# Branch sums moved from VectorE to GpSimd, a third merged block turned by VectorE, filling matmuls left out, and a new order at the turn of the layers

## What is computed

```python
def hybrid_layer(x, ...):
    proj = rms_norm(x, pre_g) @ w_in            # q,k,v,z / u,b,c,z / q,k,v,z / three gates of 2048
    o_a = dilated_mixture_attn(q_a, k_a, v_a) * silu(z_a)          # 12 heads x 128
    o_c = b_c * causal_short_conv(c_c * u_c, conv_w, conv_b) * silu(z_c)
    o_r = normed(retention(q_r, k_r, v_r)) * silu(z_r)             # 12 heads x 128
    merged = (sigmoid(g_a) * (o_a @ w_branch_a) + sigmoid(g_c) * (o_c @ w_branch_c)
              + sigmoid(g_r) * (o_r @ w_branch_r))
    return x + rms_norm(merged @ w_out, post_g)
```

## Time and profile before

| | before |
|---|---|
| median of 3 runs | 2747.36 us (2747.34 to 2747.78) |
| the profiled execution | 2747.18 us, its span 2745.3 us |
| PE busy | 2734.2 us |
| DVE busy | 1923.9 us |
| ACT busy | 1221.6 us |
| POOL busy | 27.5 us |
| DMA | 529.10 MB, 193 GB/s mean |
| mean granted TensorE clock | 0.999 |

### The profile page before, as it was taken

One profiled execution on the slowest core, in us unless ns is written; L12 is line 12 of the kernel. 1 busy time (PEld: TensorE's weight loads), 2 busy tenths in 40 slices (PEclk: granted clock), 3 DMA queues, 4 the chain that ended last, 5 costly groups with the idle time before them and its releaser, 6 DMA issues.

```text
span 2745.3 us, 30445 instructions
## 1 busy us (share of the span) xinstructions
PE 2734.2 (100%) x12270; PEld 2269.6 (83%) x12270; DVE 1923.9 (70%) x2558; ACT 1221.6 (44%) x1404; POOL 27.5 (1%) x35
## 2 busy tenths in 40 slices
PE   9999999999999999999999999999999999999998
PEld 7888888888888888888878888888888888888887
DVE  6788744767655898848567887447676558977584
ACT  6554544444443333444454545444444433434443
POOL 0000000000000000000000000000000000000000
PEclk9999999999999999999999999999999999999999
DMA  9555555555655555556565555555655565555564
GB/s 328 188 170 191 177 199 188 196 195 189 199 190 194 184 184 173 183 197 219 181 232 180 184 186 181 194 191 186 200 196 195 189 198 176 191 172 182 199 215 137
DMA packets 264732, 529.10 MB, mean 193 GB/s; under 512 B 8464, under 2 KB 8848, under 8 KB 264336
## 3 DMA queue, kind: packets, MB, share of 16 engines
q1 hardware_dynamic: 260976, 517.50, 56.9%
q10 hardware_dynamic: 2608, 4.78, 0.5%
q0 software_dynamic: 1008, 4.87, 0.5%
HBM read 522.94 MB, written 4.19 MB: 192 GB/s over the span
## 4 chain that ended last, share of the span: by engine, by line
PE 99%; DVE 0%; issue 0%; ACT 0%; DVEq 0%; POOL 0%; POOLq 0%
PE ps L649 32%; PE ps L650 32%; PE ps L651 32%; PE ps L584 0%; PE ps L602 0%; PE ps L601 0%; PE ps L604 0%; PE ps L580 0%; PE ps L565 0%; PE ps L585 0%; PE ps L579 0%; PE ps L665 0%; DVE gates L1185 0%; DVE hT_trail L1156 0%; DVE w_trail L915 0%
## 5 line engine op out<-in xcount | busy, mean ns | idle before, releaser
L915 DVE TENSOR_TENSOR w_trail<-raw,w_lead 128x1024 fp32r<-128x1024 f32 x973 | 1188.2, 1224 | 763.2 <-ACT w_lead L725 753.6
L725 ACT ACTIVATE w_lead<-raw 128x1024 fp32r<-128x1024 f32 x973 | 1028.1, 1060 | 1394.2 <-PE ps L651 1385.8
L649 PE MATMUL ps<-w_lead,hT_lead 128*128 128x512 f32 x3328 | 1299.5, 390 | 1.5 <-DVE hT_trail L1156 0.6
L650 PE MATMUL ps<-w_trail,hT_lead 128*128 128x512 f32 x3328 | 1295.5, 389 | 0.0
L651 PE MATMUL ps<-w_lead,hT_trail 128*128 128x512 f32 x3328 | 1295.4, 389 | 0.0
L649 PEld LDWEIGHTS ps<-w_lead,hT_lead 128*128 128x128 f32 x3328 | 625.0, 188 | 131.8 <-issue 2.3
L651 PEld LDWEIGHTS ps<-w_lead,hT_trail 128*128 128x128 f32 x3328 | 624.9, 188 | 130.2
L650 PEld LDWEIGHTS ps<-w_trail,hT_lead 128*128 128x128 f32 x3328 | 625.1, 188 | 128.6
L649 PE MATMUL ps<-w_lead,oT_lead 128*128 128x512 f32 x576 | 224.3, 389 | 0.0
L650 PE MATMUL ps<-w_trail,oT_lead 128*128 128x512 f32 x576 | 224.1, 389 | 0.0
L651 PE MATMUL ps<-w_lead,oT_trail 128*128 128x512 f32 x576 | 224.1, 389 | 0.0
(11 more groups left out here) (102 smaller groups left out, 783.9 us busy)
## 6 DMA issues: line engine op xcount, KB each, us to landing
raw<-w_in SPq DMA_DIRECT2D x381, 1024.0 KB, 5.2
raw<-w_out SPq DMA_DIRECT2D x32, 1024.0 KB, 5.1
raw<-w_branch_a SPq DMA_DIRECT2D x24, 1024.0 KB, 5.0
raw<-w_branch_c SPq DMA_DIRECT2D x24, 1024.0 KB, 5.0
raw<-w_branch_r SPq DMA_DIRECT2D x24, 1024.0 KB, 5.0
raw<-w_in SPq DMA_DIRECT2D x5, 512.0 KB, 5.8
gates<-x SPq DMA_DIRECT2D x4, 512.0 KB, 14.1
post_gain<-post_norm_g POOLq DMA_DIRECT2D x2, 1024.0 KB, 8.1
```

The lines of the kernel that those rows point to most:

```text
L649: pe.matmul(acc, lead[:, k, tok(t)], wl, start=(k == 0), stop=False)
L650: pe.matmul(acc, lead[:, k, tok(t)], wt, start=False, stop=False)
L725: act.activation(w_lead[:, h % SPLIT_SLOTS, :], raw[:, i % RAW_SLOTS, part:part + HALF * COLS], ACT.Copy).then_inc(lead_ready, 1)
L915: dve.tensor_tensor(w_trail[:, s, :], raw[:, i % RAW_SLOTS, part:part + HALF * COLS], w_lead[:, s, :].bitcast(F32), ALU.subtract).then_inc ...
```

## The change

`MERGE_TURNED` is 3: merged block 2 too is turned by DVE (16 more transposes a layer, again into kT, once the trail of block 0 is made), and PE transposes block 3 alone. The sums of the conv and retention branch blocks are done by POOL (`add_branch`), which waits for both tiles' products, and the turning, PE's transposes and ACT's residual DMAs wait for POOL's count instead of DVE's. ACT's gates of the retention wait for POOL's conv sums, since they overwrite `gates`. The three filling products are gone. At the seam DVE does `x_trail_of(l, 0, 1)` before `mean_y(l - 1, 1)`, and PE's `x_step` of piece (1, 0) stands between the two k of half 2, no longer behind it. Side banks are numbered by a running count over both layers (`bank_no`), since a layer now has 46 side steps, which is no multiple of four.

```diff
-MERGE_TURNED = 2
+MERGE_TURNED = 3
-FILL = 3
+        def bank_no(l, m):
+            return step_no(l, m) % SIDE_BANKS
+            def add_branch(l, mixer):
+                n0 = first_block(mixer, GROUPS) + OUT_BLOCKS
+                for j in range(OUT_BLOCKS):
+                    cols = slice(COLS * j, COLS * (j + 1))
+                    wait(*moved_out(l, n0 + j))
+                    for t in range(TILES):
+                        pool.tensor_tensor(merged[:, t, cols], merged[:, t, cols], gates[:, t, cols],
+                                           ALU.add).then_inc(merged_ready, 1)
...
+                add_branch(l, "conv")
                 for g in range(GROUPS):
                     wait(o_ssq_ready, l * GROUPS + (g + 1))
                     rstd(o_ssq, o_mean, l * GROUPS + (g + 1), o_rstd, P, 8).then_inc(o_rstd_ready, 1)
+                add_branch(l, "retention")
...
+                    if amid is not None and i == 0:
+                        x_step(*amid)
...
-                    if l == 0 and h == 0:
-                        warm(FILL)
...
-                multiply(l + 1, 2, (0,))
-                x_step(l + 1, 1, 0)
+                multiply(l + 1, 2, (0,), amid=(l + 1, 1, 0))
...
+                    if mixer == "retention":
+                        act.wait_ge(*merged_tiles(l, TILES * (j + 1)))
...
-                    if b > 0:
-                        dve.wait_ge(*moved_out(l, n))
-                        for t in range(TILES):
-                            dve.tensor_tensor(merged[:, t, cols], merged[:, t, cols], gates[:, t, cols],
-                                              ALU.add).then_inc(merged_ready, 1)
...
+                    x_trail_of(l, 0, 1)
                     mean_y(l - 1, 1)
-                    x_trail_of(l, 0, 1)
...
+                            if j > 1:
+                                dve.wait_ge(merged_trail, TILES * (MERGE_TURNED * l + j - 1))
```

More of the change, by code:

```diff
@@ L156 @@
 SIDE_STEPS = MERGE_STEP0 + MERGE_STEPS
-assert NBLOCKS % 2 == 0 and SIDE_STEPS % SIDE_BANKS == 0
+assert NBLOCKS % 2 == 0
 assert HALVES % SPLIT_SLOTS == 0 and CHUNKS % RAW_SLOTS == 0
@@ L434, in bank, with side @@
             return ps[2 * (n % 2) + t]
-        def side(m):
-            return ps[4 + m % SIDE_BANKS]
+        def side(l, m):
+            return ps[4 + bank_no(l, m)]
         def tok(t):
@@ L564, in transposes @@
                 for i, s in enumerate(sources):
-                    last = pe.transpose(side(m)[:, head(i)], s, ident)
+                    last = pe.transpose(side(l, m)[:, head(i)], s, ident)
                 last.then_inc(side_ready, 1)
@@ L599, in side_steps @@
                             h = 2 * i + hh
-                            o = side(s0 + i)[:, 2 * hh * P:(2 * hh + 2) * P]
+                            o = side(l, s0 + i)[:, 2 * hh * P:(2 * hh + 2) * P]
                             pe.matmul(o[:, 0:P], probsT[:, h, 0:P], v_sb[:, 0, head(h)], start=True, stop=True)
@@ L624, in wait_stationary, with multiply @@
                         pe.wait_ge(*step_drained(l, merge_step(k // HPB, t)))
-            def multiply(l, h, tiles=(0, 1)):
+            def multiply(l, h, tiles=(0, 1), amid=None):
                 n, k0 = place(l, h)
@@ L661, in x_step @@
                 transposes(l, x_no(t, j), [gates[:, t, head(HPB * j + i)] for i in range(HPB)])
-            def warm(times):
-                for _ in range(times):
-                    pe.matmul(side(SIDE_BANKS - 1)[:, 0:SEQ], kT[:, 0, 0:P], kT[:, 0, :], start=True, stop=True)
             pe.wait_ge(cleared, 1)
-            warm(WARM)
+            for _ in range(WARM):
+                pe.matmul(ps[4 + SIDE_BANKS - 1][:, 0:SEQ], kT[:, 0, 0:P], kT[:, 0, :], start=True, stop=True)
             for l in range(DEPTH):
@@ L768, in lead_of_step @@
                 act.wait_ge(*step_ready(l, s))
-                act.activation(dst, heads4(side(s)[:, :]), ACT.Copy).then_inc(out_lead, 1)
+                act.activation(dst, heads4(side(l, s)[:, :]), ACT.Copy).then_inc(out_lead, 1)
             def side_work(l, what, mixer, g):
@@ L801, in x_lead_of @@
                     k = HPB * j + i
-                    last = act.activation(hT_lead[:, k, tok(t)], side(m)[:, head(i)], ACT.Copy,
+                    last = act.activation(hT_lead[:, k, tok(t)], side(l, m)[:, head(i)], ACT.Copy,
                                           scale=pre_gain(l, k))
@@ L1003, in trail_of_step @@
                 dve.wait_ge(*lead_steps(l, lead_count))
-                dve.tensor_tensor(dst, heads4(side(s)[:, :]), lead.bitcast(F32),
-                                  ALU.subtract).then_inc(drained[s % SIDE_BANKS], 1)
+                dve.tensor_tensor(dst, heads4(side(l, s)[:, :]), lead.bitcast(F32),
+                                  ALU.subtract).then_inc(drained[bank_no(l, s)], 1)
             def side_work(l, what, mixer, g):
@@ L1041, in side_work @@
                                 last = dve.scalar_tensor_tensor(
-                                    z_sb[:, t, head(h)], side(s0 + i)[:, head(2 * hh + t)],
+                                    z_sb[:, t, head(h)], side(l, s0 + i)[:, head(2 * hh + t)],
                                     row_inv[:, TILES * h + t:TILES * h + t + 1], z_sb[:, t, head(h)],
                                     ALU.mult, ALU.mult)
-                        last.then_inc(drained[(s0 + i) % SIDE_BANKS], 1)
+                        last.then_inc(drained[bank_no(l, (s0 + i))], 1)
                 elif what == "values":
@@ L1155, in x_trail_of @@
                     k = HPB * j + i
-                    last = dve.scalar_tensor_tensor(hT_trail[:, k, tok(t)], side(m)[:, head(i)],
+                    last = dve.scalar_tensor_tensor(hT_trail[:, k, tok(t)], side(l, m)[:, head(i)],
                                                     pre_gain(l, k), hT_lead[:, k, tok(t)].bitcast(F32),
                                                     ALU.mult, ALU.subtract)
-                last.then_inc(drained[m % SIDE_BANKS], 1)
+                last.then_inc(drained[bank_no(l, m)], 1)
             dve.sem_inc(trail_ready, 2 * RAW_SLOTS)
```

30 lines of the change are left out of this document (15 added, 15 removed).

## The result

| | before | after |
|---|---|---|
| median of the runs beside each other | 2747.94 us (6 runs) | 2758.5 us (6 runs, 2757.14 to 2759.85) |
| ratio | | 1.0039, 95% interval 1.0029 to 1.0049 |
| profiled execution, its span | 2747.18, 2745.3 us | 2757.14, 2755.3 us |
| PE, DVE, POOL busy | | 2734.5, 1936.4, 83.8 us |

What follows compares the result with a forecast made beforehand. PE, busy 2734.2 of 2745.3 us, bounds the kernel, with DVE nearly late. On 2747.18 us: -1.74 (transposes) - 0.55 (filling) - 1.05 (seam) + 2 x 6.2 (waits) = +9.1, so 2756.2 us; range 2745.5 to 2762.

Steps and rivals of the forecast that it cites:

- DVE's list and the last sum: End of each layer: 3.9 us from DVE's products to POOL's sum makes DVE late; PE waits 6.2 us a layer.
- before halves M2+5 and M3: Where PE was to spend some of its 6.2 us wait a layer already, for late splits and block 1's trail.
- the two engines exclude each other: POOL's adds and DVE's splits with two SBUF inputs: POOL waits for the 1.22 us split between its two adds.
- PE's transposes of block 2: End of each layer: these transposes leave PE, 0.87 us in each of two layers, -1.74 us.
- The seam: Turn of the layers: earlier transposes and ACT lead release PE earlier, -1.05 us, range -2.1 to +0.2.
- The filling products: Kernel start: without them half 2 starts at 12.95, -0.55 us with a 0.7 us hole; ends 0 and -1.29.
- The clock: Loss side of dropping the filling products at the start: a clock drop behind the holes, for which nothing was counted.
- The rival: Kernel start: the 0.7 us hole lowers the clock, matmuls every 0.43 us, 2.4 us more, 2758.6 us; chance 0.04.
- a free POOL: POOL's adds run freely beside DVE's splits, a sum costs 2.7 us, total -0.5, 2746.7 us; chance 0.22.
- hidden sums: Adds of at most about 1.0 us, not held up, are ready when PE arrives: -3.3, 2743.8 us; chance 0.08.

Runs made afterwards that it cites:

- e6: Changed kernel with DVE waiting for the last sum before the split of half M3+4, so no split stands between POOL's two adds: 2755.91 us, ratio 1.0032.
- e7: Three turned blocks, new seam, no filling, DVE's products of blocks 1, 2 and trail of block 2 one half earlier, only those retention sums on POOL: 2744.56 us, 0.9989.
- e4: Kernel before with only the new order at the seam and without the filling products; two turned blocks, all sums on DVE: 2746.23 us, ratio 0.9994.
- e1: Changed kernel with all its sums back on DVE, three blocks still turned: 2751.54 us, ratio 1.0014 to the kernel before.
- e3: Kernel before with only the new order at the seam; filling products kept, two turned blocks, all sums on DVE: 2746.73 us, ratio 0.9997.
- e5: Changed kernel with eight products of constants, results unread, on PE in front of its wait for the last sum: 2754.97 us, ratio 1.0028.
- the second series: The changed kernel unaltered, run once more beside other experiments on their chip: 2758.85 us (5 runs), ratio 1.0041 to the kernel before.
- e2: Changed kernel with two merged blocks turned by DVE instead of three, sums still on POOL: 2755.28 us, ratio 1.0028.
- e11: Changed kernel with the sum of retention block 3 alone back on DVE: 2754.32 us, ratio 1.0024.

## Why the prediction was right

**DVE's list and the last sum: right, a little too slow.** Products to turning were to take 3.9 us and took 3.74 (1239.59 - 1235.85), since the handover was 0.18 instead of 0.3, and the add is 1.15 by turns, 1.2 in the sum. That the size of the add came out so near is in part luck: no row of before had one, and its bounds were 0.69 and 1.8. The forecast times of turning were 1239.5, 1257.4 and 1276.4; measured 1239.59, 1257.15 and 1275.92. The last sum was to be ready at 1295.3 and was at 1294.60. The wait "before halves M2+5 and M3" is the 0.86 us at 1282.48, half M3's, behind the trail of block 1 (and another 0.5 us in matmuls around it that start late: half M2+5 begins about 0.3 late at 1278.56, the rest is around 1282.48). Of 6.2 us a layer about 5.2 were there: the last sum at 1294.6, against 1289.1 + 0.33 for PE without any wait.

**That the two engines exclude each other: right, in both directions.** The row of before showed only POOL waiting; rows of after show a split waiting for an add (2.20 us) and an add for a split (3.53 against 2.49 us in e6). The Trainium skill (SBUF — State Buffer, Who interferes with whom) says that a VectorE instruction with two SBUF inputs and a GpSimd instruction that reads SBUF block each other, whoever is first; by that rule, this case's traces agree, down to the transposes with one input, which kept their 0.89 us. Its figure for the add (GPSIMD Engine Reference, Elementwise — side-by-side cycle accounting), about 2.6 cycles an element at 1.2 GHz, makes an estimate of 1.1 us; measured 1.15.

**PE's transposes of block 2: -1.74, right in size, but not to be had in that order.** e7 has them: it lies 3.1 below its before, e4 1.5, and the 1.6 between them are about the 1.74, though e7 changes other things as well. e1 shows the price that the forecast had put on POOL alone: with three turned blocks DVE is late without GpSimd too.

**The seam: -1.05 forecast, -0.83 measured** (-0.86 in e3). Against ACT's last square, the transposes of piece (1,0), ACT's lead, the trail and PE's release each came about 0.85 us earlier (lead 1381.44 - 6.25 = 1375.19 against 1376.04). The forecast took its own 0.7 for the transposes and carried the lead from 1376.04 to 1375.0, which is 1.04: there the sum slipped. PE's busy time in the same 20 us rose by 0.72, not by about 1.

**The filling products: -0.55 forecast, -0.50 by medians, near the noise.** In the profiled run of after half 2 starts at 13.49, as before, with a hole of 0.65: its split ran from 12.65, later than the 12.16 of before. In e4's trace it ran at 11.84, and half 2 started at 12.68. The start moves by such amounts from run to run. No lower clock behind that hole: the next matmul took 0.47, the one after 0.40.

**The clock: missing from the forecast.** The rival looked for it behind the small hole at the start, where it did not fall; its pace of 0.43 us was right. The large hole that the forecast itself predicted was not priced. Behind 3.74 us of idle time it fell, worth 1.4 us in layer 0 of the profiled run (5.93 against 4.55 in layer 1, where it did not fall) and 3.1 to 3.7 us by the medians of e5. That the rival's 2758.6 is nearly the median of 2758.5 is chance: it put the loss at another place.

**The sum.** 9.1 - 2 x 1.0 (waits) + 1.4 (clock) + 0.9 (start) + 0.2 (seam) = 9.6 of the 9.96 us measured in the profiled runs. The mechanism was the one forecast, but that the total came so near is luck in part: 2.0 us too much waiting stood against 2.5 us of clock, start and seam. The median is 1.4 us above the profiled run, which is what the clock in the second layer costs too; the lower mean clock of the other five runs points there, and the second series shows it in its trace. The rivals of a free POOL and of hidden sums fell with the wait of 3.74 us.

## What to carry to other kernels

Giving an engine's work away relieves it only if its next step doesn't wait for the result: GpSimd's sums of three retention blocks a layer cost 2.9 us where the turning waited for them, and those of two gained 2.9 us where the work of one more half lay between. Before moving elementwise work from VectorE to GpSimd, list what VectorE does meanwhile: each instruction with two SBUF inputs is delayed by a running add and delays it. And where a forecast contains a hole of several us in TensorE, price the matmuls behind it at the lower clock as well.

## What was not expected of the hardware

- GpSimd's 128x512 fp32 add of two SBUF inputs takes 1.15 us by the turns of a disturbed pair, and an undisturbed pair 2.49: 1.7 to 1.8 times VectorE's 0.69. A split that comes during an add waits for its end, and the next add waits for the split, by turns, at every pair looked at here.
- TensorE's granted clock fell around or behind idle stretches of 2.77 us (both layers of e6), 2.85 us (both of e2) and 3.74 us (layer 0 of the changed kernel's first profiled run, both layers of its second), but not always: layer 1 of the first shows 3.74 us of idle time, a granted clock of 1.00 and matmuls of 0.39 us behind. Behind the waits of 1.1 to 1.7 us in e1 and e11 it did not fall. It can fall a microsecond after the work has begun again: in e2's layer 1 PE starts at 2648.24 and the matmuls slow down at 2649.5. At the lower level matmuls are 0.43 us apart instead of 0.23, for 3 us and more each time, in e2's layer 0 for twice that.
- Products that compute nothing can pay: eight of them in front of the wait in each layer were worth 3 us, where three at the start of the kernel cost 0.5 by the medians, which is near the noise.
